# Out-projection split into two halves of K, its first half interleaved with the sliding-window attention

## The reference

```python
h = rmsnorm(x, norm1)
z = h @ w_in                      # 3848 columns, split among the mixers
a_out = chunked spatial gating    # 512 wide, causal 128x128 mixing of positions
b_out = sliding-window attention  # 1024 wide: 16 query heads, 2 key/value heads, window 128, sinks, T5 bias
c_out = mLSTM, normed and gated   # 512 wide
x = x + concat(a_out, b_out, c_out) @ w_out      # 2048 x 2048, the out-projection
x = x + ConvFFN(rmsnorm(x, norm2))               # 5632 wide, causal depthwise conv of width 3
```

```python
s = q @ k.T * 64 ** -0.5 + bias             # 128 queries x 256 keys
mx = maximum(max(s), sink)
p = exp(s - mx); p = p / (sum(p) + exp(sink - mx))
o = p @ v
```

## Time and profile before

| | |
|---|---|
| median of the runs | 2389.28 us |
| the profiled execution | 2387.86 us, of which the span is 2386.1 us |
| TensorE busy | 2280.7 us (96%), weight loads 2209.3 us |
| VectorE, ScalarE, GpSimd busy | 863.0 us (36%), 729.6 us (31%), 939.3 us (39%) |
| DMA | 215.68 MB in 323226 packets, 90 GB/s over the span |
| weight units loaded | 1024 KB each, median 5.0 to 5.5 us to landing |

### The profile page before, as it was taken

How to read it: one execution, slowest core, us unless ns; L and a number is a source line. 1 busy time by engine, 2 the same in 40 slices (tenths; PEclk the granted TensorE clock), 3 DMA queues, 4 the chain that set the end, 5 groups by cost and what they waited for, 6 DMA issues and landing times.

```text
span 2386.1 us, 45517 instructions
## 1 busy us (share of the span) xinstructions
PE 2280.7 (96%) x18446; PEld 2209.3 (93%) x18446; DVE 863.0 (36%) x1465; ACT 729.6 (31%) x1259; POOL 939.3 (39%) x735
## 2 busy tenths in 40 slices
PE   6899999877799999999999999999999999999987
PEld 6899887764699999999999999999999999999987
DVE  5111224467622244233333423343332334333332
ACT  3222232234533333232322323232232323233232
POOL 3443332210244444444444444444444444444431
PEclk9899999887899999999999999999999999999999
DMA  5732223420332333322323232232322223232223
GB/s 152 182 91 86 67 74 84 58 55 25 111 89 88 90 90 93 102 90 88 89 88 96 96 91 89 88 89 92 102 88 88 89 88 94 96 94 88 88 71 97
DMA packets 323226, 215.68 MB, mean 90 GB/s; under 512 B 11414, under 2 KB 297215, under 8 KB 322367
## 3 DMA queue, kind: packets, MB, share of 16 engines
q1 hardware_dynamic: 309987, 207.64, 28.4%
q10 hardware_dynamic: 13182, 7.24, 2.8%
HBM read 201.36 MB, written 13.85 MB: 90 GB/s over the span
## 4 chain that ended last, share of the span: by engine, by line
PE 87%; issue 5%; DVE 4%; POOL 2%; ACT 0%; ACTq 0%; DMA 0%; DVEq 0%; SPq 0%; POOLq 0%
PE ps L414 59%; PE ps L708 21%; POOL wlo L1635 2%; DVE nvar L392 1%; PE ps L666 1%; PE ps L379 1%; PE ps L656 1%; DVE sx L1435 0%; PE ps L644 0%; PE ps L768 0%; PE ps L534 0%; PE ps L498 0%; PE ps L507 0%; PE ps L506 0%; PE ps L552 0%
## 5 line engine op out<-in xcount | busy, mean ns | idle before, releaser
L1635 POOL TENSOR_TENSOR wlo<-raw,whi 128x512 fp32r<-128x512 f32 x712 | 931.4, 1311 | 1406.7 <-ACT whi L811 1278.5
L811 ACT ACTIVATE whi<-raw 128x512 fp32r<-128x512 f32 x712 | 447.7, 632 | 1343.7 <-PE ps L414 965.2
L414 PE MATMUL ps<-h_hi,whi 128*128 128x260 f32 x2816 | 395.1, 282 | 0.0
L414 PE MATMUL ps<-h_lo,whi 128*128 128x260 f32 x2816 | 393.5, 282 | 0.0
L414 PE MATMUL ps<-h_hi,wlo 128*128 128x260 f32 x2816 | 393.3, 282 | 0.0
L414 PEld LDWEIGHTS ps<-h_hi,wlo 128*128 128x128 f32 x2816 | 360.9, 188 | 0.0
L414 PEld LDWEIGHTS ps<-h_lo,whi 128*128 128x128 f32 x2816 | 360.6, 188 | 0.0
L414 PEld LDWEIGHTS ps<-h_hi,whi 128*128 128x128 f32 x2816 | 359.7, 188 | 0.4
L414 PE MATMUL ps<-act_hi,whi 128*128 128x260 f32 x1504 | 219.4, 289 | 31.0 <-POOL wlo L1635 18.5
L414 PEld LDWEIGHTS ps<-act_hi,whi 128*128 128x128 f32 x1504 | 197.1, 192 | 39.5 <-issue 38.1
L1566 DVE TENSOR_TENSOR xT<-ps,xT 128x520 f32<-128x520 f32 x160 | 111.9, 699 | 287.9 <-PE ps L708 286.6
(11 more groups left out here) (296 smaller groups left out, 1458.3 us busy)
## 6 DMA issues: line engine op xcount, KB each, us to landing
raw<-in_w_up SPq DMA_DIRECT2D x88, 1024.0 KB, 5.2
raw<-in_w_down SPq DMA_DIRECT2D x44, 1024.0 KB, 5.0
raw<-in_w_in SPq DMA_DIRECT2D x30, 1024.0 KB, 5.0
raw<-in_w_out SPq DMA_DIRECT2D x16, 1024.0 KB, 5.5
x_spill<-xT SPq DMA_DIRECT2D x1, 4160.0 KB, 24.6
xT<-x_spill SPq DMA_DIRECT2D x1, 4160.0 KB, 12.4
xtok<-in_x_prompt SPq DMA_DIRECT2D x4, 1024.0 KB, 8.7
out_y_prompt<-ytok SPq DMA_DIRECT2D x4, 1024.0 KB
```

Source lines behind the costliest of these rows:

```text
L414: mm = nc.tensor.matmul(ps[:, bank + h, 0:NH], w[:, k, c, :], x[:, 4 * c + k, h * NH:(h + 1) * NH], start=(k == 0 and kind == 0 and c == 0 ...
L811: nc.scalar.activation(whi[:, k, :, :], rawq(k, slot), ACT.Copy)\
L1635: nc.gpsimd.tensor_tensor(wlo[:, k, :, :], rawq(k, u), whi[:, k, :, :].bitcast(F32), ALU.subtract).then_inc(w_lo, 1)
```

## The change

- **Bias rows.** 33 copies instead of 129 (`BR = 32`), issued by SP, which now issues the two loads of the gating mixer as well. A bias tile, one transfer before, is read back in four of 32 partitions.
- **Two halves of K.** The 16 column tiles of the out-projection are worked off in pairs. For units 30 to 37, quarters 0 and 1 are the mLSTM rows of w_out for two tiles, quarters 2 and 3 the gating mixer's rows for the same tiles; VectorE adds the sum to x (`add_half`). Units 38 to 45 do the same with the attention's rows. The number of matmuls is the same: 64 quarters of 24.
- **Rounds.** The barrier and the loops are gone. Each engine's list runs 39 rounds: round m has, where they exist, the values of step m-7, the turning of step m-5, the scores of step m-3, and then one dense quarter. Rounds 5, 8, 12, 18 and 25 have no quarter. Round 2 begins with the sample's keys, which wait for the caches. The attention's buffers move into tiles of `zT` that are free by then, and the maximum is kept negated, so that a copy and a sign change a step go.
- **SP's list** between the input projection and the rounds: 11 of the 16 tiles of x, the two caches, sinks, new rows, bias tiles, the last 5 tiles of x, five stores, weights.
- **GpSimd** gates the mLSTM output and splits off the gating mixer's low parts.

The diff, cut to its core:

```diff
-    BIAS_PITCH = (P + 1) * 384
-    bias_rows = nc.dram_tensor("bias_rows", [16, P + 1, 384], F32, kind="Internal").ap()
+    BR = 32
+    BIAS_PITCH = (BR + 1) * 384
...
+    U_LATE = U_OUT + KC // 2
+    STEPS, AHEAD = 32, 3
+    ROUNDS = STEPS + AHEAD + 4
+    FREE_ROUNDS = (5, 8, 12, 18, 25)
+    DENSE = [m for m in range(ROUNDS) if m not in FREE_ROUNDS]
+    assert len(DENSE) == 2 * KC + 2
+    dense_in = {m: d for d, m in enumerate(DENSE)}
+    x_early = 11
+    EARLY_STORES = 12
     DIAG = [0, 512, 896, 1152]
     SCORE_AT = [(5, 0), (6, 0), (7, 0), (6, 384)]
...
+        def dense(d):
+
+            u, k = U_OUT + d // 4, d % 4
+            late, tile, half = d >= 2 * KC, 2 * (d // 4) + k % 2, k // 2
+            if half == 0:
+                if tile == 0:
+                    pe.wait_ge(s("b_kv"), 1)
+                elif tile == 1:
+                    pe.wait_ge(z_free, Z_N + 2)
+                elif tile < KC + 2:
+                    pe.wait_ge(s("o_half"), tile - 1)
...
+            pe.wait_ge(s("b_lo") if late else (s("a_lo") if half else s("c_lo")), 4 + 4 * half if late else 4)
+            pe.wait_ge(w_lo, 4 * u + (k + 1))
+            half_tile(k, half, bx if late else ax)
+
+        def half_tile(k, half, x):
+
+            b = 2 * (k % 2)
+            for kind, (w, p) in enumerate(((whi, 0), (whi, 1), (wlo, 0))):
+                for c in range(4):
+                    for h in range(2):
+                        mm = nc.tensor.matmul(ps[:, b + h, 0:NH], w[:, k, c, :],
+                                              x[:, p, 4 * half + c, h * NH:(h + 1) * NH],
+                                              start=(half == 0 and kind == 0 and c == 0),
+                                              stop=(half == 1 and kind == 2 and c == 3))
+            mm.then_inc(w_used, 1)
...
+        def sample(m):
+            if m == 2:
+                pe.wait_ge(slice_read, LAST_SLICE - SLICE0 + 1)
+                pe.wait_ge(s("kc_in"), 16 * 4)
+                for b in range(S):
+                    t = nc.tensor.transpose(ps[:, 4 + b // 4, (b % 4) * P:(b % 4 + 1) * P], kc_[:, b, :], ident[:])
+                t.then_inc(s("b_kct"), 1)
...
-        barrier(pe, 1)
-
-
-        for u in range(2):
-            pe.wait_ge(z_free, U_OUT + u + 1)
-            unit_mm(4 * (U_OUT + u), 2 * u,
-                    before=(lambda k: pe.wait_ge(mix_lo, 4 * (k + 1))) if u == 0 else None)
...
+        for m in range(ROUNDS):
+            sample(m)
+            for part, at in ((pv, AHEAD + 4), (turn, AHEAD + 2), (qk, AHEAD)):
+                if 0 <= m - at < STEPS:
+                    part(m - at)
+            if m in dense_in:
+                dense(dense_in[m])
+
+        dense(2 * KC + 2)
+        dense(2 * KC + 3)
+        with pe.Fori(1, KC // 2) as j:
+            for k in range(4):
...
-        act.wait_ge(s("rel_read"), 1)
-        act.dma_start(bias_rows, brow[:].rearrange("h (a w) -> h a w", a=1).broadcast_to([16, P + 1, 384]))\
-            .then_inc(s("rel_out"), 16)
-        act.dma_start(ws[:], io["a_spatial_w"].rearrange("l g t s -> t (l g) s")).then_inc(s("ws_in"), 16)
-        asb, asw = io["a_spatial_b"], io["a_spatial_w"]
-        act.dma_start(w00[:], bass.AP(tensor=asw.tensor, offset=asw.offset, ap=[[0, P], [P * P, 4], [1, 1]])).then_inc(s("a_in"), 16)
+        asb = io["a_spatial_b"]
...
-                act.dma_start(kc_[1:P, :, :], io["cache_swa_k"][0, :, 1:P].rearrange("b w h d -> w b (h d)")).then_inc(s("kc_in"), 16)
...
                 for q in range(2):
...
+        def late_hi(u):
+            act.wait_ge(s("b_of"), 4 * u + 4)
+            if u == 0:
+                act.wait_ge(s("b_o8_read"), 1)
+                act.wait_ge(s("chunk_out"), 16)
+            nc.scalar.activation(bx[:, 0, u, :], zT[:, Z_BQ + u, :], ACT.Copy).then_inc(s("b_hi"), 1)
+
+        for m in range(2, ROUNDS + 1):
+            if m - 1 in dense_in:
+                out_hi(dense_in[m - 1] + 4)
+            sample(m)
+            if 0 <= m - AHEAD - 2 < STEPS:
+                read_turn(m - AHEAD - 2)
+            if 0 <= m - AHEAD < STEPS:
+                exps(m - AHEAD)
+            if m >= AHEAD + 8 and (m - AHEAD - 8) % 4 == 0:
+                late_hi((m - AHEAD - 8) // 4)
 
...
+        def add_half(d):
+            tile = 2 * (d // 4) + d % 4 - 2
+            if tile == 0:
+                dve.wait_ge(spilled, 32)
+            if tile == x_early:
+                dve.wait_ge(spilled, 48)
+            dve.wait_ge(w_used, 4 * U_OUT + d + 5)
+            x = halves(xT[:, tile, :])
+            tt(x, pair(2 * (tile % 2)), x, add).then_inc(s("o_half"), 1)
+
+        def late_lo(u):
+            dve.wait_ge(s("b_hi"), u + 1)
+            tt(bx[:, 1, u, :], zT[:, Z_BQ + u, :], bx[:, 0, u, :].bitcast(F32), sub).then_inc(s("b_lo"), 1)
+
+        for m in range(ROUNDS + 1):
+            sample(m)
+            if 0 <= m - AHEAD < STEPS:
+                score(m - AHEAD)
+            if 0 <= m - AHEAD - 1 < STEPS:
+                scale(m - AHEAD - 1)
+            if 0 <= m - AHEAD - 4 < STEPS:
+                read_o(m - AHEAD - 4)
+            if m >= AHEAD + 8 and (m - AHEAD - 8) % 4 == 0:
+                late_lo((m - AHEAD - 8) // 4)
+            d = dense_in.get(m - 1)
+            if d is not None and d % 4 >= 2 and d < 2 * KC:
+                add_half(d)
+
         link(nc.vector.memset(ssum[:], 0.0))
 
         def one(ap):
             return ap.rearrange("p a n -> p (a n)")
...
-        barrier(pool, 1)
-        split_pairs(Z_N // 2, U_ALL // 2)
+
+        def split(u, k):
+            pool.wait_ge(w_hi, 4 * u + k + 1)
+            nc.gpsimd.tensor_tensor(wlo[:, k, :, :], rawq(k, u % 2), whi[:, k, :, :].bitcast(F32),
+                                    ALU.subtract).then_inc(w_lo, 1)
+
+        for k in range(4):
+            split(U_OUT, k)
+            if k == 0:
+                pool.wait_ge(s("c_sig"), 1)
+                pool.wait_ge(slice_read, 27 - SLICE0 + 1)
+            nc.gpsimd.tensor_tensor(zT[:, Z_CO + k, :], zT[:, Z_CV + k, :], zT[:, Z_CO + k, :], ALU.mult)                .then_inc(s("c_mix"), 1)
+        for c in range(4):
+            pool.wait_ge(s("a_hi"), c + 1)
+            nc.gpsimd.tensor_tensor(ax[:, 1, 4 + c, :], zT[:, Z_AU + c, :], ax[:, 0, 4 + c, :].bitcast(F32), ALU.subtract)                .then_inc(s("a_lo"), 1)
...
+        sp.dma_start(ws[:], asw.rearrange("l g t s -> t (l g) s")).then_inc(s("ws_in"), 16)
+        sp.dma_start(w00[:], bass.AP(tensor=asw.tensor, offset=asw.offset, ap=[[0, P], [P * P, 4], [1, 1]])).then_inc(s("a_in"), 16)
+        sp.wait_ge(s("rel_read"), 1)
+        sp.dma_start(bias_rows, brow[:].rearrange("h (a w) -> h a w", a=1).broadcast_to([16, BR + 1, 384]))\
+            .then_inc(s("rel_out"), 16)
         for a, b, col, unit in ((2, 6, COL_C, Z_CQ), (6, 8, COL_AV, Z_AV), (8, 9, COL_BK, Z_BK),
...
+        def load_out(u, col, late, split):
+
+            sp.wait_ge(w_lo, split)
+            for k in range(4):
+                row = (4 + 4 * (k // 2) if late else (12, 0)[k // 2]) * P
+                src = w_out[row:row + 4 * P, bass.ds(col + (k % 2) * P, P)].rearrange("(c p) n -> p c n", p=P)
+                sp.dma_start(rawq(k, u), src).then_inc(raw_in[u], 16)
+
+        for v in range(2):
+            load_out(v, 2 * P * v, False, 4 * (U_OUT + v) - 4)
+
+        def bias_tile(u):
+
+            for a in range(P // BR):
+                sp.dma_start(bst[BR * a:BR * a + BR, u % 2, :, :],
+                             bass.AP(tensor=bias_rows.tensor, offset=P - 1 - BR * a + 2 * u * BIAS_PITCH,
+                                     ap=[[383, BR], [BIAS_PITCH, 2], [1, 256]])).then_inc(bias_in[u % 2], 16)
+
+        def x_back(a, b):
+            sp.dma_start(xT[:, a:b, :].rearrange("p c n -> p (c n)"), spill[:, a * N:b * N]).then_inc(spilled, 16)
+
+        sp.wait_ge(slice_read, LAST_SLICE - SLICE0)
+        sp.wait_ge(s("cst_out"), 32)
+        x_back(0, x_early)
         sp.wait_ge(w_used, USED_IN)
+        sp.dma_start(kc_[1:P, :, :], io["cache_swa_k"][0, :, 1:P].rearrange("b w h d -> w b (h d)")).then_inc(s("kc_in"), 16)
+        sp.dma_start(vc_[1:P, :, :], io["cache_swa_v"][0, :, 1:P].rearrange("b w h d -> w b (h d)")).then_inc(s("kc_in"), 16)
+        sinks = io["b_sinks"]
+        sp.dma_start(sinkbc[:], bass.AP(tensor=sinks.tensor, offset=sinks.offset, ap=[[0, P], [1, 16]])).then_inc(s("b_in"), 16)
...
-            if n >= 2:
-                sp.wait_ge(s("b_sc_free"), 4 * n - 2)
-            sp.dma_start(bst[:, u % 2, :, :], bass.AP(tensor=bias_rows.tensor, offset=P - 1 + 2 * u * BIAS_PITCH,
...
-            load_pair([cols_of(w_out, i * (2 * P) + (u - U_OUT) * P) for u in range(2)], i * 8 - 4)
+        sp.dma_start(kc_[0:1, :, :], kv8[:, 0, :]).then_inc(s("kc_in"), 16)
+        sp.dma_start(vc_[0:1, :, :], kv8[:, 1, :]).then_inc(s("kc_in"), 16)
...
+        bias_tile(1)
+        sp.wait_ge(slice_mm, LAST_SLICE - SLICE0 + 1)
```

(42 more changed lines are left out.)

515 lines of the change are left out of this document (224 added, 291 removed).

## The result

The changed kernel takes 2403.52 us (median of 5 runs, 2402.13 to 2404.75), the kernel before 2389.14 us (5 runs, 2384.92 to 2392.45): ratio 1.0064, 95% interval 1.0049 to 1.0079. The forecast was 2388, no change. The time lies inside the range of 2368 to 2406, but it moved where no move was forecast: slower had a chance of 0.27.

What follows compares the result with a forecast made beforehand. TensorE, busy 96% of the span, was taken as the bound, so only its idle stretches could yield time. The terms -19.0 + 0.7 + 16.8 gave -1.5 us, hence 2388 us against the median, range 2368 to 2406.

Steps and rivals of the forecast that it cites:

- Part 1: Bias rows near 50 us: TensorE's 17.75 us wait and the restart behind it go; -19.0 us.
- Part 2: Slice 21 of the input projection: four more transposes and a ScalarE copy nobody waits for; +0.7 us.
- rival B: Rounds: VectorE's way, slowed beside GpSimd, outgrows the quarter and TensorE waits in dense rounds; 2420 us, chance 0.09.
- Part 3: Sample's caches after the input projection: loaded by about one DMA engine, leaving TensorE idle about 55 us, until 586.
- Part 4: Rounds, from TensorE's release: 163.4 us to quarter 33's end, out-projection done at 837.9 against 821.1; +16.8 us.
- the waits behind the rounds without a quarter: Five rounds without dense work leave VectorE's way uncovered: 5 x 2.1 = 10.5 us of TensorE waiting.
- 1.66 each: TensorE's time for each of 24 full attention steps in the rounds; with 8 short ones at 0.95, 47.5 us.
- The restart at the low clock: 2.0: One slow start of TensorE, counted once between its release and the end of quarter 33; 2.0 us.
- the 1.0 us for the weights of unit 2: In the rounds, a wait for weights that SP issues behind 22 other transfers; one us.
- A: Ahead of the rounds: the caches arrive by 534 us and the long TensorE wait does not come; 2334 us, chance 0.09.
- C: Projection, 60 to 110 us: the early wait returns in SP's queue, gain 9 us less; 2397 us, chance 0.08.
- D: Rounds: the clock stays at 1.2 GHz, some 140 us more; 2528 us, chance 0.02.

Runs made afterwards that it cites:

- e1: Kernel before with only the early part: 33 bias-row copies, their write and the two gating loads issued by SP, tiles read in four pieces; 2372.22 us.
- e9: Kernel before with 33 bias-row copies, the write and the two gating loads still issued by ScalarE; 2378.43 us.
- e10: Kernel before with all 129 bias-row copies, but the write and the two gating loads issued by SP; 2391.23 us.
- e7: e3 with four small gating operations of VectorE moved from slice 28 to 27 and a constant root on ScalarE at the start of slice 24; 2349.47 us.
- e3: Changed kernel with each sample cache loaded in two pieces, 112 and 15 partitions instead of 127; 2353.35 us.
- e6: e3 with TensorE's waits in the rounds and ahead of quarter 34 filled with matmuls by zeros; 2351.53 us.
- e2: Changed kernel with the early part undone: 129 bias-row copies and both gating loads issued by ScalarE, tiles in one piece; 2423.90 us.

## Why the forecast was wrong, by its own steps

- **Part 1** was right: 19.0 forecast, 17.7 measured alone (e1). Fewer copies give 11.7 of it by themselves (e9), the other issuer nothing by itself (e10).
- **Part 2 failed in size**: 0.7 us forecast, and slice 29 begins another 5.0 later. "Four more transposes [...] +0.7 us. The other moved evictions lie beside slice 29" counted what the change adds to each engine, and not what it puts beside something else or takes from ahead of it. e7 shows two costs. GpSimd's gating, new in slice 28, runs beside four VectorE operations that take 0.87 us alone: 2.74, and the wait ahead of slice 29 is 3.96 us, not 1.98. Ahead of the root in slice 24 ScalarE no longer issues a cache, and its table load, 1.28 us, now comes behind the wait for VectorE instead of ahead of it: 3.8 us of wait, not 2.7 as in e1. Together 3.1 of the 5.0. The other 2 I can't assign, and one profile scatters by more: five kernels with the same code up to slice 29 begin it at 506.21, 503.98, 506.09, 505.61 and 509.56 us (changed kernel, e3 to e6). Part of the scatter is the clock. In the changed kernel slice 28 begins at the low clock, in e3 at the full one, behind the same wait, and from there to slice 29 it is 20.87 us and 18.22:

```profile
485.34 1.97 PE L570 MATMUL ps<-ident,zT 128*128 128x128 f32 x8 [3.57 <-DVEq L1404]
```

```profile
485.76 1.09 PE L570 MATMUL ps<-ident,zT 128*128 128x128 f32 x8 [3.55 <-DVEq L1404]
```

  The collision of VectorE and GpSimd is rival B's: I looked for it in the rounds, where it brought no wait, and not in the projection, where it cost 2.0 us.
- **Part 3** was right to 1.3 us: 52.54 us of idle TensorE, from the partition count of two loads (e3).
- **Part 4 failed in size, and carries most of the miss**: 172.6 us for 163.4. The quarters (3.07), the change into them (0.2) and the waits behind the rounds without a quarter (7.8, and 2.5 in rounds 6 and 7, of 10.5) came out. Two terms did not. "1.66 each": the rates of the parts came for scores and values from two of them in a row, and single ones between other work cost more: 0.70 us for four steps (a short one among them, 1.17 for 0.95), 5.6 for 32. This is read from the trace; no run isolates it. "The restart at the low clock: 2.0", once: in rounds 7, 9 and 19 the clock is low again behind a wait, about 1.5 us each (5.20 us from the scores at 606.79 to 611.99, where e6 has 3.70), 4.5 in all. The two make 10.1, more than the 9.2; the 1.0 us for the weights of unit 2 did not come, for no wait for weights stands there. The tail has another restart, 4.50 us for quarter 34 instead of 2.87; that is most of its 2.2.
- **The rivals.** A, B, C and D did not come. B's clause "TensorE waits in dense rounds" did not come either: behind a round with a quarter stands one wait, 0.98 us in round 7, for VectorE's read of the sample's output. Of D a part is there: the clock is full over most of the rounds (1.00 over 690 to 742 us), but not behind three of the waits.
- **The balance.** The forecast set a gain of 19 and a cost of 17.5 against each other. The gain was 17.7; the cost was 34.0 alone (e2) and 31.3 on top of e1. Of its 0.72 it gave 0.60 to a time at most 8 us above the one that it found, and 0.12 to more. That the time still lies inside the range is in part luck: part 2 and the restarts had no bounds, and the room came from those of other terms. "[...] without the hold it would end at 784, 37 us early" fails by the same terms: e3 is 18.9 us under e1, with 3.7 us of the wait left. Four of the five deviations have one sign: steps were priced at the rate of equal parts in a row, restarts were counted once, and what runs beside what was not looked at.
